# Paired attention on 768 keys: score rows of both maps packed into three PSUM banks, the turned weights alternating between two banks

## What is computed

```python
def _diff_attention(dq, dk, dv, lam):
    s = jnp.einsum('bqhjd,bkhjd->bhjqk', dq, dk).astype(jnp.float32) * ATTN_SCALE
    p = jax.nn.softmax(s, axis=-1)
    a = (p[:, :, 0] - lam * p[:, :, 1]).astype(dv.dtype)
    return jnp.einsum('bhqk,bkhe->bqhe', a, dv)

def _gqa_attention(gq, gk, gv):
    s = jnp.einsum('bqhgd,bkhd->bhgqk', gq, gk).astype(jnp.float32) * ATTN_SCALE
    p = jax.nn.softmax(s, axis=-1).astype(gv.dtype)
    return jnp.einsum('bhgqk,bkhd->bqhgd', p, gv)
...
            dk_all = jnp.concatenate([dk, cdk], axis=1)
            gk_all = jnp.concatenate([gk, cgk], axis=1)
```

## Time and profile before

| | us |
|---|---|
| median of 3 runs | 3904.27 |
| the three runs | 3896.54 to 3905.62 |
| the profiled execution | 3903.54 |
| its span in the trace | 3901.8 |
| PE busy in the span | 3594.7 (92%) |
| DVE / ACT busy | 1915.3 (49%) / 1397.7 (36%) |

### The profile page before, as it was taken

One profiled execution on the slowest core, in us unless ns is written; L12 is line 12 of the kernel. 1 busy time (PEld: TensorE's weight loads), 2 busy tenths in 40 slices (PEclk: granted clock), 3 DMA queues, 4 the chain that ended last, 5 costly groups with the idle time before them and its releaser, 6 DMA issues. The chain is left out here.

```text
span 3901.8 us, 47626 instructions
## 1 busy us (share of the span) xinstructions
PE 3594.7 (92%) x18674; PEld 2766.3 (71%) x18674; DVE 1915.3 (49%) x2912; ACT 1397.7 (36%) x2388; POOL 131.4 (3%) x90
## 2 busy tenths in 40 slices
PE   6989897979999999997897999999997999989998
PEld 2879896855677778873774567778886776667767
DVE  0756565665554354441475654444443346433553
ACT  2454433324443322222323444332222425334352
POOL 0000000010000000000001000010001000000000
PEclk9999998999999999998998999999998999989999
DMA  8425354320122322336330112323332211222112
GB/s 317 148 91 162 123 164 135 102 70 28 44 65 86 93 70 93 97 108 249 126 96 33 44 49 65 103 65 97 93 97 94 64 61 49 76 87 69 62 44 92
DMA packets 97405, 371.72 MB, mean 95 GB/s; under 512 B 11184, under 2 KB 11440, under 8 KB 95280
## 3 DMA queue, kind: packets, MB, share of 16 engines
q1 hardware_dynamic: 97200, 368.82, 29.1%
HBM read 357.25 MB, written 11.53 MB: 95 GB/s over the span
## 5 line engine op out<-in xcount | busy, mean ns | idle before, releaser
L368 DVE TENSOR_TENSOR w_lo<-w_raw,w_hi 128x1024 fp32r<-128x1024 f32 x527 | 645.1, 1224 | 753.2 <-ACT w_hi L358 752.6
L382 PE MATMUL banks<-h_hi,w_hi 128*128 128x512 f32 (+2 forms) x2040 | 790.2, 387 | 26.3 <-DVE h_lo L1038 9.9
L384 PE MATMUL banks<-h_hi,w_lo 128*128 128x512 f32 (+2 forms) x2040 | 748.5, 367 | 0.0
L383 PE MATMUL banks<-h_lo,w_hi 128*128 128x512 f32 (+2 forms) x2040 | 748.0, 367 | 0.0
L358 ACT ACTIVATE w_hi<-w_raw 128x1024 fp32r<-128x1024 f32 x545 | 572.6, 1053 | 358.9 <-DMA w_raw<-in_stream 348.5
L382 PEld LDWEIGHTS banks<-h_hi,w_hi 128*128 128x128 f32 (+1 forms) x2040 | 390.8, 192 | 113.9 <-issue 33.8
L384 PEld LDWEIGHTS banks<-h_hi,w_lo 128*128 128x128 f32 (+1 forms) x2040 | 390.0, 191 | 65.1
L383 PEld LDWEIGHTS banks<-h_lo,w_hi 128*128 128x128 f32 (+1 forms) x2040 | 391.5, 192 | 54.2 <-issue 3.8
L382 PE MATMUL banks<-merged_hi,w_hi 128*128 128x512 f32 (+1 forms) x960 | 345.8, 360 | 11.7 <-DVE mid L1245 7.8
L384 PE MATMUL banks<-merged_hi,w_lo 128*128 128x512 f32 (+1 forms) x960 | 341.7, 356 | 0.0
L383 PE MATMUL banks<-merged_lo,w_hi 128*128 128x512 f32 (+1 forms) x960 | 341.5, 356 | 0.0
(11 more groups left out here) (322 smaller groups left out, 4869.9 us busy)
## 6 DMA issues: line engine op xcount, KB each, us to landing
w_raw<-in_stream SPq DMA_DIRECT2D x593, 512.0 KB, 3.6
w_whole<-in_stream SPq DMA_DIRECT2D x48, 512.0 KB, 8.9
x_kept<-x SPq DMA_DIRECT2D x4, 2048.0 KB, 7.8
x<-x_kept SPq DMA_DIRECT2D x4, 2048.0 KB, 8.4
dft_table<-in_dft SPq DMA_DIRECT2D x2, 2048.0 KB, 8.6
x<-in_x SPq DMA_DIRECT2D x1, 2048.0 KB, 11.1
out_x<-x SPq DMA_DIRECT2D x8, 256.0 KB, 4.4
late_consts<-in_consts SPq DMA_DIRECT2D x1, 1152.0 KB, 5.4
```

Source lines behind the costliest of these rows:

```text
L368: (by or self.nc.vector).tensor_tensor(self.lo[:, c], self.raw[:, c], self.hi[:, c].bitcast(F32), ALU.subtract)\
L382: self.nc.tensor.matmul(out, w_hi, x_hi, start=start, stop=False)
L383: self.nc.tensor.matmul(out, w_hi, x_lo, start=False, stop=False)
L384: mm = self.nc.tensor.matmul(out, w_lo, x_hi, start=False, stop=stop)
```

## The change

For a stage whose keys fill three banks for two lanes exactly (768 keys; the 256-key stage keeps its code), the two score rows lie behind each other in banks 0 to 2. Lane 0 has bank 0 and the first half of bank 1, lane 1 the second half of bank 1 and bank 2. Lane 1's 512 latent keys are cut in two matmuls of 256, so a step has five score matmuls in place of four. Both lanes write bank 1, and a new semaphore, `att_shared_bank` (`self.cleared`), keeps them apart in time: lane 0's second matmul waits until lane 1's first is done. Bank 3, now free, takes every second fill of transposes, and a fill waits for the copy of the fill before the last one.

```diff
-        self.wide = -(-n_keys // BANK) * BANK
+        self.tight = 2 * n_keys % BANK == 0 and n_keys > BANK
+        self.wide = n_keys if self.tight else -(-n_keys // BANK) * BANK
         self.flat = K.ps[:, 0:2 * self.wide // BANK, :].rearrange("p b n -> p (b n)")
+        self.turn_banks = (4, 3) if self.tight else (4,)
+        self.cleared = S("att_shared_bank")
...
+                def score(lane, part, a, b):
+                    keys, at = group.keys[lane][part]
+                    mm[lane] = nc.tensor.matmul(self.scores_at(lane, at + a, at + b),
+                                                group.queries[lane][:, i * P:(i + 1) * P], keys[:, a:b], start=True, stop=True)
+                if self.tight:
+                    score(0, 0, 0, BANK)
+                    score(1, 0, 0, BANK // 2)
+                    mm[1].then_inc(self.cleared.sem, 1)
+                    score(1, 0, BANK // 2, BANK)
+                    score(1, 1, 0, BANK // 2)
+                    pe.wait_ge(self.cleared.sem, self.cleared.at(s + 1))
+                    score(0, 1, 0, BANK // 2)
+                else:
+                    for part in range(len(group.keys[0])):
+                        for lane in range(2):
+                            score(lane, part, 0, group.keys[lane][part][0].shape[1])
...
-                        if x > 0:
-                            pe.wait_ge(self.turned_out.sem, self.turned_out.at(x))
+                        if x >= len(self.turn_banks):
+                            pe.wait_ge(self.turned_out.sem, self.turned_out.at(x - len(self.turn_banks) + 1))
...
-                                mm = nc.tensor.transpose(K.ps[:, 4, at:at + P],
+                                mm = nc.tensor.transpose(K.ps[:, self.turn_banks[x % len(self.turn_banks)], at:at + P],
```

More of the change, by code:

```diff
@@ L1422, in act @@
                         nc.scalar.activation(self.T[:, lane:lane + lanes, a:b, i * P:(i + 1) * P],
-                                             K.ps[:, 4, 0:lanes * (b - a) * P].rearrange("p (l k n) -> p l k n", l=lanes, n=P),
+                                             K.ps[:, self.turn_banks[x % len(self.turn_banks)], 0:lanes * (b - a) * P].rearrange("p (l k n) -> p l k n", l=lanes, n=P),
                                              ACT.Copy).then_inc(self.turned_out.sem, 1)
@@ L1484, in close @@
         n_diff = sum(g.diff for g in self.groups)
-        for s, c in ((self.scored, 2 * n), (self.negmax, n), (self.exped, 2 * n), (self.inverse, n),
+        for s, c in ((self.scored, 2 * n), (self.cleared, n if self.tight else 0), (self.negmax, n), (self.exped, 2 * n), (self.inverse, n),
                      (self.scaled, 2 * n_diff * self.nq), (self.weighted, (2 * u - n_diff) * self.nq), (self.turned, self.fill_at[-1]),
```

## The result

The changed kernel takes 3911.6 us (median of 14 runs, 3907.42 to 3921.99) against 3904.5 us for the kernel before (14 runs, 3896.54 to 3910.57). The ratio is 1.0023 with an interval of 1.0014 to 1.0032: slower by 5 to 12 us. The time lies in the range given (3889 to 3917), on the other side of no change, 2 us under rival A's 3914.

The account below looks back on a forecast made before the run. The prediction took PE to set the pace in both latent stages. Scores at 0 and 5.6 us won from the fill waits, taken from the median 3904.27, gave 3898.7 us, with a whole range of 3889 to 3917.

Parts of the forecast that it names:

- rival A: Score steps: matmuls complete in program order, so the new wait costs 0.33 us in each of 64; 3914 us, chance 0.33.
- What bounds the kernel: Both latent stages: PE sets the pace, so each microsecond it loses or wins there counts as one of the total.
- The fill waits: Transposes waiting for ACT's copies: all eight waits per stage go, 6.8 us lost per stage, 13.6 us in both.
- What comes next instead: PE meets its next waits, mostly for exponentials, earlier; 2.8 us won per stage, 5.6 in all, bounds 3.4 and 13.6.
- The split of the 512 columns: Lane 1's scores: the extra matmul adds no columns and its weight loads are hidden; priced at nothing.
- The new wait: Lane 0's last score matmul waits for lane 1's first; ready at 0.86 us, row half free at 0.96; cost nothing.
- the upper end: The new wait's bound if the short matmul is not reported done before the long one: 0.33 us per step, 21 us.
- the lower end: The new wait's bound taken in the forecast: nothing, since lane 0's row half is busy until 0.96 us anyway.
- Rival B: Score steps: passes in strict turns between lanes, lane 1 ending 0.21 us late in each of 64; 3912 us, chance 0.10.
- Rival C: Latent stages: score waits take nothing back, so all 13.6 us are won; 3890.7 us, chance 0.08.

Follow-up runs that it names:

- the scores alone: The change with one bank instead of two for the turned weights; 3919.16 us, ratio 1.0045 to the kernel before.
- the two good orders: The change with lane 1's short matmul issued first (3899.44, 3894.83 us), and the change with lane 0's 512 columns cut too (3895.0, 3897.6 us).
- the six pieces: The change with lane 0's 512 columns cut too, three pairs of 256 columns, lanes alternating; 3895.0 us, ratio 0.9976 to the kernel before; again 3897.6 us.

## Why the prediction was wrong

**What bounds the kernel** was right. The PE paced both stages in every kernel, and what a step lost or won came out in the run time: for the scores alone 18.2 us more in the stages at the same clock, beside a ratio of 1.0045 (17.6 us).

**The fill waits** went, all eight per stage, as the order said.

**What comes next instead** was sized right: 5.6 us, with 2.8 per stage. At the same clock a stage is 2.6 us shorter than before where the step is not lengthened (359.9 to 357.3), and 2.9 to 3.1 shorter than with the new order and one turned bank; the four runs of the two good orders are 5 to 9 us faster. That it fits so closely is in part luck, since the prediction took half of what it had left without a row for the half. In the long step more is won, 3.8 us per stage (369.0 to 365.2). The exponentials then have more time until they are awaited, which would explain it; I did not test that by itself. The place where the rest comes back was named (exponentials, 5.6 to 8.2 us); that DVE's weights take 1.3 us too was not.

**The split of the 512 columns** was priced at nothing. The step takes 1.491 us as before with one matmul more and the short one first, 1.496 with one more in the order of the change without its wait, and 1.496 with two more in the six pieces. So it costs between nothing and 0.005 us a step.

**The new wait is the step that failed.** The prediction said: "The wait ends 0.10 us before it could hurt, cost nothing." Its picture of the matmuls was right. The short one does end 0.70 us after the step's start (1078.58) beside a long one that runs to 1.12. What was wrong is the silent next step, that the end of a matmul's record is the time of its signal. The signal waits for every older matmul. It came at 1.15, the weight load at 1.19, and the step took 1.82 us, which is what the upper end gave: 0.33 a step, 21 us. The upper end had the last matmul of lane 0 start at 1.29; it starts at 1.20, and the 0.11 of its weight load stands inside its first pass and not ahead of it, with the same sum. The reason given for taking the lower end was that each lane goes at its own row half's pace. This holds for starts and ends, and it said nothing about signals. For that, the trace of before had no row. With the bounds 0 and 21 us and the gain of 5.6, the side of the result hung on this one term, so it deserved more than a third.

**Rival A** is what happened, through half of its mechanism: signals in program order, ends not. Its price was right. Of the 21 us, about 3 were absorbed (21.2 less the 18.2 at the same clock); the prediction had allowed up to 11.

**Rival B** (passes in turns) is out: in the change lane 1's second pass comes 0.32 after the first (1077.885 and 1078.205 in the trace), 0.21 before lane 0's. **Rival C** is out too, since the waits for exponentials rose.

The Trainium skill's rule (page "TensorE: Matmul & The Clock Gate", section "Part 3: Packing small matmuls") pointed the right way, and the prediction gave it a third. It says more than these runs show. Without a wait, a matmul written behind one of the other row half started 0.01 us ahead of it (1078.299 and 1078.311). By the modelled ends the short one was over 0.42 us before an older long one. What is in program order is the signal, and for a wait that is what counts.

## What to carry to other kernels

When matmuls on different row groups run side by side and one of them signals, put that one first in the program; a longer, older one beside it holds the signal until its own end. Such a hole does not show as idle time, because the other row group is busy: compare the length of a step, not PE's idle time. And where a change is to give 6 us and takes an unmeasured wait 64 times, a swap of two lines in a side kernel tells its price before the rest is argued.

## What the runs showed of the hardware

- Signals of matmuls leave in program order, between the two row halves too: 0.45 us after the short matmul's record had ended (1078.58 to 1079.03), 0.03 after the end of the older one. With the short one older: 0.01 after its own end. Both hold in all 64 steps.
- Starts on two row halves are not in program order: without a wait, lane 0's last matmul, written last, loaded its weights 0.01 us after the long one's second pass had begun and started 0.01 us before the other lane's.
- An extra float32 matmul that adds no columns costs 0 to 0.005 us per step where its weight load is covered (1.491 and 1.496 against 1.491). An uncovered load makes the first pass 0.11 longer (0.32 against 0.21).
- A latent stage lasts 357.4 us with 6.8 us at the lower granted clock and 354.2 with none (the six pieces again).
